# A GLU product by seven block products, with half of its gate multiplications on GpSimd

## The reference

```
y_ssm = gelu(y_ssm + ssm_d * u)
y_ssm = y_ssm * sigmoid(y_ssm @ w_glu)            # w_glu: 1024 x 1024
mixed = sigmoid(g_s) * (y_ssm @ p_ssm) + sigmoid(g_a) * (att @ p_att)
```

## Time and profile before

| | |
|---|---|
| median of three runs | 1138.98 us (1138.76 to 1139.98) |
| profiled execution | 1138.88 us, its span 1137.0 us |
| busy in the span: PE, PE weight loads, DVE, ACT, POOL | 99%, 92%, 63%, 51%, 22% |
| mean granted TensorE clock | 0.997 |
| HBM read and written | 110.73 MB, 16.84 MB |

### The profile page before, as it was taken

How to read it: one execution, slowest core, us unless ns; L and a number is a source line. 1 busy time by engine, 2 the same in 40 slices (tenths; PEclk the granted TensorE clock), 3 DMA queues, 4 the chain that set the end, 5 groups by cost and what they waited for, 6 DMA issues and landing times.

```text
span 1137.0 us, 20248 instructions
## 1 busy us (share of the span) xinstructions
PE 1122.8 (99%) x8160; PEld 1041.2 (92%) x8160; DVE 720.1 (63%) x1171; ACT 581.3 (51%) x1108; POOL 254.1 (22%) x211
## 2 busy tenths in 40 slices
PE   9999999999999999999999999999999999999997
PEld 8999999999779999998889988899889889989986
DVE  6565999997784644554774563574868347635745
ACT  6563676654797533343665352454327416614742
POOL 1066888871110000000000000000044025023203
PEclk9999999999999999999999999999999999999999
DMA  9443435546103543354556203214332323242242
GB/s 217 134 143 78 112 92 173 143 139 177 49 1 92 181 132 90 120 170 117 166 166 206 61 33 122 82 39 167 102 84 75 112 74 100 73 125 71 68 159 84
DMA packets 154140, 128.76 MB, mean 113 GB/s; under 512 B 15712, under 2 KB 127264, under 8 KB 153728
## 3 DMA queue, kind: packets, MB, share of 16 engines
q1 hardware_dynamic: 142560, 114.76, 34.3%
q10 hardware_dynamic: 11488, 12.70, 3.3%
HBM read 110.73 MB, written 16.84 MB: 112 GB/s over the span
## 4 chain that ended last, share of the span: by engine, by line
PE 88%; ACT 5%; DVE 3%; issue 1%; ACTq 1%; POOL 1%; DVEq 0%; POOLq 0%
PE gp L2432 27%; PE gp L2838 14%; PE sp L2838 13%; PE gp L3148 6%; PE sp L3148 6%; PE gp L2915 4%; PE gp L2742 3%; PE gp L3108 2%; PE sp L3074 1%; ACT sc L1246 1%; PE sp L2742 1%; PE sp L2945 1%; PE gp L2479 1%; ACT raw L1059 1%; PE gp L2453 1%
## 5 line engine op out<-in xcount | busy, mean ns | idle before, releaser
L1684 DVE TENSOR_TENSOR wL<-wraw,wH 128x1024 fp32r<-128x1024 f32 x139 | 181.2, 1306 | 151.6 <-ACT wH L972 149.0
L972 ACT ACTIVATE wH<-wraw 128x1024 fp32r<-128x1024 f32 x139 | 146.1, 1054 | 199.5 <-PE sp L2838 57.5
L2432 PE MATMUL gp<-aH,wH 128*128 128x288 f32 (+2 forms) x800 | 174.3, 300 | 0.0
L2432 PE MATMUL gp<-aL,wH 128*128 128x288 f32 (+2 forms) x800 | 171.9, 297 | 0.0
L2432 PE MATMUL gp<-aH,wL 128*128 128x288 f32 (+2 forms) x800 | 171.9, 297 | 0.0
L920 POOL TENSOR_TENSOR comb<-wraw 128x512 f32<-128x512 f32 x12 | 15.7, 1312 | 637.9 <-DMA wraw<-in_w_ff 580.8
L2432 PEld LDWEIGHTS gp<-aH,wH 128*128 128x128 f32 x800 | 130.0, 190 | 2.0 <-issue 1.8
L2432 PEld LDWEIGHTS gp<-aL,wH 128*128 128x128 f32 x800 | 130.4, 190 | 0.0
L2432 PEld LDWEIGHTS gp<-aH,wL 128*128 128x128 f32 x800 | 130.3, 190 | 0.0
L2838 PE MATMUL gp<-wH,fH 128*128 128x512 f32 x208 | 81.3, 391 | 0.0
L2838 PE MATMUL gp<-wL,fH 128*128 128x512 f32 x208 | 81.0, 390 | 0.0
(11 more groups left out here) (549 smaller groups left out, 2839.4 us busy)
## 6 DMA issues: line engine op xcount, KB each, us to landing
wraw<-in_w_ff SPq DMA_DIRECT2D x64, 512.0 KB, 4.4
wraw<-in_w_in SPq DMA_DIRECT2D x36, 512.0 KB, 4.7
gates_scratch<-sq ACTq DMA_DIRECT2D x16, 288.0 KB, 2.3
gate<-gates_scratch SPq DMA_DIRECT2D x16, 288.0 KB, 4.2
wraw<-in_p_att SPq DMA_DIRECT2D x8, 512.0 KB, 4.1
wraw<-in_w_glu SPq DMA_DIRECT2D x8, 512.0 KB, 4.0
wraw<-in_p_ssm SPq DMA_DIRECT2D x8, 512.0 KB, 3.7
wraw<-in_w_out SPq DMA_DIRECT2D x8, 512.0 KB, 4.0
```

Of the source, the lines that this page charges most:

```text
L972: s_.activation(halves_of(t, j)[0][:], wraw[w][:], ACT.Copy).then_inc(wh_done, 1)
L1684: v.tensor_tensor(low[:], wraw[w][:], high[:], ALU.subtract).then_inc(wl_done, 1)
L2432: last = mm(gp[:, b + h, 0:n], w[:, k, :], y[:, k, c0:c0 + n], start=(k == 0 and w is wH[s] and y is xh), stop=(k == KT - 1 and w is wL[s]))
```

## The change

GLU slabs 0 and 1 stay as they were. Slabs 2 to 7 become three pairs (n = 0, 1, 2) of seven products. The four sums of data blocks (S1, S2, S4, S3) are formed by POOL from `z` when the first cut of it is made, during the attention projection, and split by ACT and DVE at the start of the GLU. POOL forms each pair's sums of weight blocks. Of each pair, DVE multiplies the odd slab (3, 5, 7) by its gate and POOL the even one (2, 4, 6), after the odd one's cut. The sigmoid of the pair's first quarter, `raw[:, 0, 0:HT]`, is taken within the pair, behind `out_12`. Pair 1's weights get two raw buffers of their own, in place of the gate rows; the loads of gate rows 8 to 11 and of the memory rows move behind them. The pairs of weight halves are renamed from `p_ssm` on (`wH2`, `wL2`), some semaphores of the start are merged into one, and counters are shifted; these edits are not shown.

The core of the diff (on SP, POOL, ACT, DVE and PE, in this order):

```diff
+        def glu_place(n, name):
+            return {"RA": (2, 0, 8), "T1": (0, 0, 4), "T3": (0, 4, 8), "T2": (3, 0, 4), "RB1": (1, 0, 4),
+                    "T4": (3 if n % 2 else 1, 4, 8)}[name]
+
+        def glu_place_free(n, name):
+
+            if name == "T4":
+                return (g_count(T_GLU + 2), g_count(T_GLU), glu_product_at(0, "T4"))[n]
+            if n == 0:
+                return g_count(T_GLU + {"RA": -1, "T2": 0, "T1": 1, "T3": 1, "RB1": 2}[name])
+            return glu_product_at(n - 1, "RA1" if name == "RA" else name)
...
                     sp.wait_ge(wl_done, t - 1)
+                elif t in (T_GLU + 4, T_GLU + 5):
+                    sp.wait_ge(evac_dve, 8)
+                elif t in (T_GLU + 6, T_GLU + 7, T_PSSM, T_PSSM + 1):
+                    n = 0 if t < T_PSSM else 2
+                    sp.wait_ge(wl_done, glu_operand_at(n, "RB1"))
+                    sp.wait_ge(comb_ready, glu_comb_at(n, "T4"))
...
+                    if t0 == T_GLU and j < 3:
+
+                        load_gate_rows(5 + j)
+                    if t0 == T_GLU and j == 7:
+                        sp.wait_ge(wl_done, glu_operand_at(1, "RB1"))
+                        sp.wait_ge(comb_ready, glu_comb_at(1, "T4"))
+                        for n in (8, 9):
+                            load_gate_rows(n)
+                    if t0 == T_PSSM and j == 1:
+                        for n in (10, 11):
+                            load_gate_rows(n)
+                    if t0 == T_PSSM and j == 4:
+
+                        sp.wait_ge(gemm_done, g_count(T_PSSM))
                         for i in range(2):
                             sp.dma_start(memr[i][:], a["mem_prompt"][0, i * P:(i + 1) * P, :]).then_inc(mem_loaded[i], 16)
...
                 g.tensor_copy(rdenx[:], rden[:, n % 2, :].unsqueeze(2).broadcast_to([P, 8, HD])).then_inc(rdenx_ready, 1)
 
+            pool.wait_ge(in_h, IN_Y + 1)
+            pool.wait_ge(gemm_done, T_PATT + 1)
+            for name, first, second, op in (("S1", z_block(0, 1), z_block(1, 1), ALU.subtract),
+                                            ("S2", timed(zsum["S1"]), z_block(0, 0), ALU.subtract),
+                                            ("S4", z_block(1, 0), timed(zsum["S2"]), ALU.add),
+                                            ("S3", z_block(0, 0), z_block(0, 1), ALU.subtract)):
+                if name in ("S2", "S4"):
+                    pool.wait_ge(sum_ready, 1 if name == "S2" else 2)
+                g.tensor_tensor(timed(zsum[name]), first, second, op).then_inc(sum_ready, 1)
...
+            def glu_combine(n):
+
+                ra, rb = glu_raw(n)
+
+                def free(name):
...
+            def glu_gated(n):
+
+                j = 2 + 2 * n
+                natural = "p (c s) -> p c s"
+                pool.wait_ge(out22_done, n + 1)
+                pool.wait_ge(in_l, IN_Y2 + j + 1)
+                g.tensor_tensor(sq[:, 0].rearrange(natural, s=SB), raw[:, 0].rearrange(natural, s=SB), by_time(z[:, j, :]),
+                                ALU.mult).then_inc(raw_ready, 1)
+
+            glu_combine(0)
+            glu_combine(1)
+            glu_gated(0)
+            glu_combine(2)
+            glu_gated(1)
+            glu_gated(2)
...
-                split_h(T_GLU + j + AHEAD, j + AHEAD)
-                act.wait_ge(gemm_done, T_GLU + j + 1)
-                s_.activation(halves(raw[:, j % 2]), result(j), ACT.Sigmoid).then_inc(evac_act, 1)
-                cut_h(aH[:, j, :], sq[:, j % 2])
-                if j in (1, 2):
-                    gate_sig(7 + j)
+            z_sum_h("S2")
+            glu_operand_h(0, "T2")
+            z_sum_h("S1")
+            glu_sigmoid(0)
+            glu_operand_h(0, "T1")
+            glu_operand_h(0, "T3")
+            glu_cut_h(0)
+            z_sum_h("S3")
+            glu_operand_h(0, "RB1")
+            glu_operand_h(0, "T4")
+            for n in range(3):
+                if n:
+                    glu_cut_h(2 * n + 1)
+                glu_keep(n, "p1")
+                if n:
+                    if n < 2:
+                        glu_operand_h(n + 1, "RA")
+                    else:
+                        split_h(T_PSSM, 0)
+                    glu_cut_h(2 * n)
+                else:
+                    z_sum_h("S4")
+                    glu_sigmoid(1)
+                act.wait_ge(*glu_join_at(n, "12"))
+                s_.activation(raw[:, 0, 0:HT], raw[:, 0, 0:HT], ACT.Sigmoid)
+                glu_keep(n, "p16")
+                if n == 0:
+                    glu_cut_h(1)
+                    glu_operand_h(1, "RA")
+                if n < 2:
+                    glu_operand_h(n + 1, "T2")
+                else:
+                    split_h(T_PSSM + 1, 1)
+                glu_keep(n, "p5")
+                if n < 2:
+                    glu_operand_h(n + 1, "T1")
+                    glu_operand_h(n + 1, "T3")
+                else:
+                    gate_sig(8)
+                    gate_sig(9)
+                act.wait_ge(*glu_join_at(n, "11"))
+                s_.activation(raw[:, 1], raw[:, 1], ACT.Sigmoid).then_inc(evac_act, 1)
+                if n < 2:
+                    glu_operand_h(n + 1, "RB1")
+                    glu_operand_h(n + 1, "T4")
+                else:
+                    split_h(T_PSSM + 2, 2)
+                act.wait_ge(gemm_done, glu_product_at(n, "T4"))
+                s_.activation(raw[:, 0, HT:TT], PAIR_BANK[n % 2][0], ACT.Sigmoid).then_inc(out22_done, 1)
+            glu_cut_h(7)
+            glu_cut_h(6)
...
+            def glu_gated(j):
+
+                n = (j - 2) // 2
+                if j < 2:
+                    dve.wait_ge(evac_act, ACT_BEFORE[T_GLU] + j + 1)
+                elif j % 2:
+                    dve.wait_ge(evac_act, ACT_BEFORE[T_GLU] + 2 + n + 1)
+                else:
+                    dve.wait_ge(out22_done, n + 1)
                 dve.wait_ge(in_l, n_in[0])
                 v.tensor_tensor(sq[:, j % 2].rearrange(natural, s=SB), raw[:, j % 2].rearrange(natural, s=SB), by_time(z[:, j, :]),
                                 ALU.mult).then_inc(raw_ready, 1)
...
+
+            def glu_out_12(n):
+
+                dve.wait_ge(*glu_kept_at(n, "p1"))
+                dve.wait_ge(gemm_done, glu_product_at(n, "RA1"))
+                dve.wait_ge(raw_ready, 2 * n + (2 if n else 1))
...
+            for n in range(3):
+                if n:
+                    glu_gated(2 * n + 1)
+                    if n < 2:
+                        glu_operand_l(n + 1, "RA")
+                    else:
+                        split_l(T_PSSM, 0)
+                    glu_cut_l(2 * n + 1)
+                else:
+                    z_sum_l("S4")
+                glu_out_12(n)
+                if n == 0:
+                    glu_gated(1)
+                    glu_operand_l(1, "RA")
+                    glu_cut_l(1)
+                else:
+                    glu_cut_l(2 * n)
+                if n < 2:
+                    glu_operand_l(n + 1, "T2")
+                    glu_operand_l(n + 1, "T1")
+                else:
+                    split_l(T_PSSM + 1, 1)
+                glu_out_21(n)
+                if n < 2:
+                    glu_operand_l(n + 1, "T3")
+                glu_out_11(n)
+                if n < 2:
+                    glu_operand_l(n + 1, "RB1")
+                    glu_operand_l(n + 1, "T4")
+                else:
+                    split_l(T_PSSM + 2, 2)
+            glu_gated(7)
+            glu_cut_l(7)
+            glu_cut_l(6)
...
+                left = {"RA0": (bH, bL, 0, lower), "RA1": (bH, bL, 4, lower), "T2": (zsH["S2"], zsL["S2"], 0, lower),
+                        "T1": (zsH["S1"], zsL["S1"], 0, lower), "T3": (bH, bL, 0, upper),
+                        "RB1": (zsH["S4"], zsL["S4"], 0, lower), "T4": (bH, bL, 4, upper)}
+                bank = dict(zip(PRODUCTS, (PAIR_BANK[n % 2][i] for i in (0, 1, 0, 2, 0, 2, 0))))
+                for name in PRODUCTS:
+                    operand = {"RA0": "RA", "RA1": "RA"}.get(name, name)
+                    pe.wait_ge(wl_done, glu_operand_at(n, operand))
...
+                        pe.wait_ge(suml_done, {"T2": 1, "T1": 2, "T3": 3, "RB1": 4}[name])
+                    if name == "T2":
+                        pe.wait_ge(*glu_kept_at(n, "p1"))
+                    if name == "T3":
+                        pe.wait_ge(*glu_kept_at(n, "p16"))
+                    if name == "RB1":
+                        pe.wait_ge(*glu_kept_at(n, "p5"))
+                    if name == "T4":
+                        pe.wait_ge(*glu_join_at(n, "21"))
...
+            for j in range(2):
+                gemm(T_GLU + j, j, bH, bL, (evac_dve, 8 + j - 1), IN_Y if j == 0 else None)
+            pe.wait_ge(evac_dve, 8)
+            glu_products(0)
+            pe.wait_ge(evac_act, ACT_BEFORE[T_GLU] + 2)
+            glu_products(1)
+            glu_free(0)
+            glu_products(2)
+            glu_free(1)
```

(37 more changed lines are left out.)

263 lines of the change are left out of this document (181 added, 82 removed).

## The result

The changed kernel takes 1172.04 us (median of four runs, 1170.53 to 1173.06) where the kernel before takes 1139.32: a ratio of 1.0286, 95% interval 1.0268 to 1.0304. I had forecast 1159 and a range up to 1168. The direction was right, the size was not: +33 where I had +20.

The account below looks back on a forecast made before the run. TensorE was taken to bound the kernel (88% of the span). Terms 1.5 + 4.0 + 6.4 + 5.2 + 6.4 + 1.7 = 25.2, less 4.9 saved, gave +20.3: 1159 us, range 1149 to 1168.

Parts of the forecast that it names:

- Sums of z (in the attention projection): Attention projection: POOL's sums hold DVE's products, so slab 5's weight is cut late; taken 1.5 us (0 to 5).
- the short sums: Attention projection: with POOL's sums at 2.9 us each, slab 5's weight is not late; no wait.
- The clock: After the 6.4 us stand at the end: granted clock falls, 3.4 us at 0.50; taken 1.7 us (0 to 3.4).
- lie under later waits: Pairs 1 and 2: clock falls there may happen but are hidden by later waits, so no term was added.
- Pairs 0, 1 and 2: GLU slabs 2 to 7: TensorE waits of 4.0, 6.4 and 5.2 us on top of the pairs' matmuls.
- the one at RB1 of pair 1: Pair 1: p5 stands behind T2's copy, which waits for POOL's sums of pair 2; 1.1 us.
- T3's wait: Pair 2: p16 comes at 11.65 against 7.2, behind p_ssm's split, slab 5's cut and POOL's gate product; 4.4 us.
- The end: First p_ssm slab, after six steps: late third-slab load, split, gate products and cuts make TensorE wait 6.4 us.
- GpSimd's prices: POOL's strided products in the GLU and projection: gate product taken 1.9 us, each sum of z 3.9.
- the first rival: POOL pays the stride in full, gate product 2.2 and sum 4.5 us: +25 to +27, 1165 us; chance 0.20.
- The matmuls: GLU: six slabs go (38.40 us), three pairs come (33.48 us); -4.9 us if nothing waits.
- The covers hold, faster: Pairs: p16 comes before T3 in every pair, so the whole -4.9 us stays: 1134 us; chance 0.05.

Follow-up runs that it names:

- sums_alone: Kernel before the change plus only GpSimd's four sums of z, at the change's point and unused: 1152.6 us, ratio 1.0117.
- sums_late: Changed kernel with GpSimd starting the four sums of z after the projection's fifth slab, four slabs later: 1161.25 us, ratio 1.0193.
- fillers: Changed kernel with matmuls on a constant put into TensorE's waits in the pairs and p_ssm: 1172.64 us, ratio 1.0289.
- s3_after_cuts: The reordered kernel with the last sum, S3, moved behind VectorE's last cut of z and the orders adapted: 1137.45 us, ratio 0.9983.
- the reordered kernel: Changed kernel with sums after the fifth slab, even gates on VectorE, end-of-pair-3 load and split moved, ScalarE's and VectorE's pair programs reordered: 1136.27 us, ratio 0.9970.
- sums_fill: Changed kernel with GpSimd writing a constant in place of the four sums of z: 1159.81 us, ratio 1.0185.
- sums_copy: Changed kernel with GpSimd copying each sum's first input instead of forming the sum: 1162.83 us, ratio 1.0211.
- tail: Changed kernel with gate rows 10 and 11 loaded behind p_ssm's third weight, and that weight's split behind the last GLU cuts: 1166.08 us, ratio 1.0243.

## Why the prediction was wrong

**The step that failed** is "Sums of z (in the attention projection)", "Taken 1.5 (0 to 5)". The length of the four rounds was right as a whole: I had a round of 3.9 and some 1.0, and the four rounds took 19.23 us, 4.8 each; the held VectorE products were foreseen. What I asked was only when VectorE cuts the weight of slab 5, and even that came out 2.5 us late and 0.3 more a slab on, so that by its own working the term was 2.5 and more; the 1.5 lies between that and the none of the short sums. I did not ask what else stands in VectorE's queue behind the held products: the evacuation of the projection's PSUM banks, for which TensorE waits from slab 4 on (L3116). That wait had 2.0 us to spare before the change, where slab 1's evacuation ended at 368.47 and slab 4 began at 370.47:

```profile
367.99 0.48 DVE L1996 TENSOR_TENSOR m<-sp,gsig 128x320 f32<-128x320 f32 x1
```

The first held product alone, 5.4 us for 1.2, ate 4.2. sums_alone, with nothing but the sums, costs 13.2 us; sums_late, which moves nothing but the sums, gives back 10.8.

**The clock** was taken at 1.7, for one fall behind the last stand. The rows above add up to some 33 us at half clock (1.2 of 2.4 GHz) in the windows shown (the mean's distance from 1, times the window, twice). Where TensorE sets the time, in the projection, that cost 2.4 and 2.9 us (sums_alone). Behind the last stand it cost 2.7 (58.8 less 51.2 and the stand of 4.9): the window from 482 to 490 alone has 6.2 us at half clock, where I had taken 3.4 from a stretch without a stand. In the pairs it cost nothing that the fillers could give back, as the prediction had it for pairs 1 and 2 ("lie under later waits"). So the term at the end was 1.0 too small, and the 5.3 of the projection, part of its 13.5, had no term at all.

**Pairs 0, 1 and 2** were taken at 4.0, 6.4 and 5.2 over 11.16: 15.2, 17.6 and 16.4 us. They took 15.5, 17.2 and 18.9, by the starts of RA0. The waits of pairs 1 and 2 sit where the prediction put them, but smaller; the one at RB1 of pair 1 shows only in fillers (0.8), where TensorE comes to it at full clock. For pair 2, where I put T3's wait at 4.4, the trace has 4.1 behind this chain (p_ssm's split on ScalarE, GpSimd's gate product, ScalarE's cut; p16 follows at 464.95):

```profile
459.17 1.07 ACT wH L1102
...
462.30 1.69 POOL sq L1018
464.01 0.61 ACT aH L1152
```

```profile
465.49 0.58 PE L3149 MATMUL sp<-bH,wH 128*128 128x288 f32 x1 [4.08 <-ACT p L1451]
```

The 2.5 us by which pair 2 was longer than forecast are the clock's (fillers: 16.3), and they lie under the wait in p_ssm, which is as much longer in fillers.

**The end** was taken at 6.4 for the wait and 1.7 for the clock; the p_ssm slabs grew by 7.6, 4.9 of it the wait. Load, split, gate product and cuts come in the order foretold, and the load of the third slab took 6.3 where I had 5.7:

```profile
468.14 6.30 DMA wraw<-in_p_ssm
474.47 1.07 ACT wH L1102
...
479.53 1.69 POOL sq L1018
...
481.96 0.77 DVE aL L1916
```

**GpSimd's prices.** The gate product took 1.68 to 1.69 (taken 1.9), 1.18 times the contiguous 1.42 of the earlier trace rows, about half of the surcharge that I read there. The Trainium skill, GPSIMD Engine Reference, section 7 (Performance pitfalls for Q7 kernels), would have it half as much again, by estimate 2.1; at this shape, with one strided input, the trace does not agree. The sums were 4.06 and 3.89 with one strided input and 5.43 and 5.73 with two, each with what it waited for VectorE in it. Where no VectorE product from SBUF ran just before them, the two with two strided inputs took 4.46 (S1 in sums_late) and 4.77 (S3 in s3_after_cuts): the stride in full, as the first rival (4.5) and, nearly, the page's half (4.3 in the prediction) had it. The others, counted from the end of the VectorE product ahead of them, took 3.05. That the mean comes out near the 3.9 that I took is luck. 0.2 us too much on three gate products is under 1 us in all.

**The matmuls**, -4.9, were right, and they show only where nothing stands: in the reordered kernel the third pair ends 80.2 us after the first cut of y, where the eighth slab ended at 83.5; the 1.3 that S3 adds to the projection, with the 1.16 us stand in it, keep the rest. The rival "The covers hold, faster" I gave 0.05, with no way to it but a misread wait. For the queues as they stand in the change that holds; with the queues of the reordered kernel p16 comes before T3 in every pair, at 1136.3 us where the rival had 1134.

What stays open: the two stands and the half clock of the projection come and go together (with neither stand, in sums_late and sums_fill, and with the one of 2.45 us in sums_copy, the clock is 1.00 from 372 to 392 us), and no run separates them, since no PSUM bank is free there for fillers. An order of VectorE's queue in the projection with the evacuations ahead of the products that GpSimd holds was not tried.

## What to carry to other kernels

When a new instruction holds an engine, list everything that stands behind the held ones in that engine's queue, PSUM evacuations first, and who waits for each; pricing the one consumer that comes to mind missed 12 us here. Put idle-engine work where the engine that it blocks has slack (four slabs later was worth 10.8 us), and within a stage put first in each queue what the bounding engine needs next: the same work in another order turned +9 us into -3. Here a clock fall cost time only where TensorE itself was the chain.

## What the runs showed of the hardware that was not expected

- GpSimd writing a constant for 4.3 us left VectorE's two-input products at 1.2 us; copying one SBUF input held them for the whole copy, as a two-input sum did.
- The same stand of 2.64 us at T3 of pair 1 was followed by a granted clock of 0.72 in the changed kernel and of 1.00 in sums_late. Six microseconds from that matmul on, changed kernel first:

```profile
446.87:452.87 6.00, 5.49 (x28) 0.72 0.00 0
```

```profile
436.10:442.10 6.00, 4.20 (x28) 1.00 0.00 0
```

The length of the last stand alone does not tell whether the clock falls: ahead of this one the changed kernel had stood for 1.9 us at 429.74 and run below full clock behind it, and sums_late had waited no longer than 1.64 us since the pairs began, at 1.00 throughout. Earlier stands do not tell it either: tail and sums_fill both stood 1.9 us at T3 of pair 0 with a clock of 1.00 behind it, and 2.6 at T3 of pair 1; in the six microseconds from there the clock was 1.00 in tail (from 446.67) and 0.76 in sums_fill (from 432.85). What decides it stays open.
